# A fused kernel's first block reordered: adaLN columns summed by rows, the S5 branch moved beside the RWKV chain

## The chip, the cores and the metric

One Trainium2 chip, one core. The metric is the device time of one execution, in microseconds (us). The kernel before took 1775.86 us, the median of three runs (1773.12 to 1776.78).

## The reference

The program computes a first block (adaptive norm, input projection, an RWKV-7 time mix beside an S5 state-space mix, output projection, feed-forward) and two further layers of another kind, all in float32 on 512 tokens of width 1024. The change touches the first block only.

```python
ada = silu(c) @ w_ada + b_ada                       # 1024 x 6144
sh_m, sc_m, g_m, sh_f, sc_f, g_f = jnp.split(ada, 6, axis=-1)
h = modulate(rms_norm(x), sh_m, sc_m)               # h * (1 + sc) + sh
proj = h @ w_in                                     # 1792 columns z, 512 columns u
z = z + mu_shift * (z_prev - z)
y_rwkv = rwkv7_time_mix(z, ...)
y_s5 = s5_mix(u, ...)
x = x + g_m * (concatenate([y_rwkv, y_s5]) @ w_out)
h = modulate(rms_norm(x), sh_f, sc_f)
ffn = (silu(h @ w_gate) * (h @ w_up)) @ w_down
x = x + g_f * ffn

# s5_mix: complex powers of abar, then states, then the output
bbar_re = coef_re[..., None] * b_re - coef_im[..., None] * b_im
bbar_im = coef_re[..., None] * b_im + coef_im[..., None] * b_re
_, _, s_re, s_im = lax.associative_scan(_ssm_combine, (a_seq_re, a_seq_im, bu_re, bu_im), axis=0)
y = einsum(c_re, s_re) - einsum(c_im, s_im) + d_skip * ug
zz = gelu(y);  out = zz * sigmoid(zz @ w_glu + b_glu);  out = rms_norm(out) * gain

# rwkv7_time_mix, per token and head
sa = einsum(S, a_t);  S = S * w_t + sa * b_t + v_t * k_t;  y = einsum(S, r_t)
```

## The kernel before, in words

The program is written by hand for each engine. Classes Tensor, Vector, Scalar, Pool and Sync each emit one engine's instructions in their own order (PE, DVE, ACT, POOL and the queue that issues DMAs). They meet on semaphores only, so an instruction that waits holds all that is written behind it on its engine.

**Weights.** All dense weights stream as 234 units of 512 KB, each eight blocks of 128x128, through a ring of four buffers: `Sync.load` (L2794) may fetch unit u+4 when unit u has been eaten. A unit of a dense product is split into a high part (ACT, `unit`, L2035) and a low part (DVE, a subtraction on L1168), and a block is then three matmuls (`mms`, L355). Units in `WHOLE`, those of `w_ada`, are not split.

**First block.** `Tensor.ada_tiles` (L451) makes shift and scale (sh_m, sc_m) from 16 units, each block a matmul with one column; a float32 matmul shows as two instructions in the trace. DVE builds the S5 tables meanwhile (`s5_tables`). Then come the norm h1, the four u tiles of the input projection by rows, the S5 matrices (`s5_matrices`, L514), and a hand-written string ORDER that sets 14 z tiles (`in_proj`, L537) beside the S5 branch (`s5_apply`, L545: the states as a scan on DVE, the outputs yg on PE, a gated unit with dense tiles, a norm). After it `rwkv` (L595) runs: the preparation in two halves, grams (L643), the inverse of unit lower-triangular matrices in five levels (L710), steps (L742) and a scan over eight chunks (L773). The other 32 `w_ada` units are row-summed on DVE beside it (`Vector.ada_columns`, L1333: a scalar times a 128x1024 row added to a sum, L1176), and PE turns each sum into eight columns. Then group norm (L839), output projection (L866), norm h2 and the feed-forward (L879) of 22 tiles.

Helpers record many operations under one line: L350 is every matmul, L353 a transpose, L1168 every tensor-tensor operation of DVE, L1176 its scalar-tensor-tensor, L2592 POOL's tensor-tensor, L2035 ACT's copy, L2032 its other functions. An "arena" is SBUF memory addressed by hand, "b" a PSUM bank, "ring" the raw weights and ring2/ring_55 their low parts, X the residual, H/HR the normed input, cst and par constants, nst the norm's small values.

## Time and profile before

| | |
|---|---|
| median of three runs | 1775.86 us |
| the profiled execution's own time | 1779.91 us |
| its span | 1778.1 us |
| mean granted TensorE clock | 0.928 of full |
| PE busy | 1574.7 us (89%) in 10056 instructions |
| DVE busy | 866.0 us (49%) in 1390 |
| ACT busy | 566.6 us (32%) in 976 |
| POOL busy | 311.4 us (18%) in 245 |
| first matmul of the feed-forward | 574.3 us after the span's start |

Busy is the time in which an engine executed. The profiled execution is 4.05 us above the median, and its own time is 1.8 us over its span. Share of busy time is an average over the whole program, so it says little about the first block, which is the third of the span that is changed.

### The profile page before, as it was taken

What the parts mean: (1) busy time and instruction counts of PE and PEld (TensorE: products, weight loads), DVE (VectorE), ACT (ScalarE), POOL (GpSimd) and SP (SyncE); (2) the same over time, 40 slices, a digit from 0 to 9 for tenths busy, and PEclk for the clock granted to TensorE, in tenths of its full rate; (3) what the DMA queues carried; (4) which work ended last, traced back from release to release, by engine and by line L of the source; (5) the groups of instructions that cost most, each with busy time, mean ns of one, the idle gap of its engine ahead of it and who ended that gap; (6) DMA issues with size and microseconds to landing.
All of it is one profiled execution on the core that took longest, in us unless ns stands there. A gap on an engine that the chain in (4) does not pass through costs nothing.

```text
span 1778.1 us, 23936 instructions
## 1 busy us (share of the span) xinstructions
PE 1574.7 (89%) x10056; PEld 1245.4 (70%) x10056; DVE 866.0 (49%) x1390; ACT 566.6 (32%) x976; POOL 311.4 (18%) x245
## 2 busy tenths in 40 slices
PE   8987697376888999999998999997898989998889
PEld 8875585166866888888886677765676668775767
DVE  7726602876644433332335455445644455444652
ACT  2222114521142322222222443323442443322351
POOL 0000000654110011110001233223210223322110
PEclk9998768689898999999998999999898999999999
DMA  6356103123402222223222111120123112220121
GB/s 248 119 106 84 48 24 95 53 76 127 143 27 81 83 95 95 95 95 124 95 95 83 37 59 60 60 71 25 60 71 113 48 36 75 69 69 26 60 72 70
DMA packets 50362, 141.03 MB, mean 79 GB/s; under 512 B 12624, under 2 KB 17360, under 8 KB 49744
## 3 DMA queue, kind: packets, MB, share of 16 engines
q1 hardware_dynamic: 50256, 139.50, 25.0%
q8 instruction: 80, 1.31, 0.3%
q14 instruction: 26, 0.21, 0.0%
HBM read 134.80 MB, written 4.69 MB: 78 GB/s over the span
## 4 chain that ended last, share of the span: by engine, by line
PE 65%; DVE 10%; ACT 7%; issue 4%; POOL 2%; DMA 1%; SPq 0%; DVEq 0%; ACTq 0%; POOLq 0%
PE b L350 63%; ACT arena L2032 4%; DVE arena L1176 2%; DVE arena L1168 2%; DVE ring L1168 2%; PE b L353 1%; POOL arena L2592 1%; ACT ring L2035 1%; DVE arena L1862 1%; POOL arena L2595 1%; ACT arena L2035 1%; DVE arena L1995 1%; ACT L2032 1%; DVE arena L1820 1%; ACT tile L2035 0%
## 5 line engine op out<-in xcount | busy, mean ns | idle before, releaser
L350 PE MATMUL b<-tile,ring 128*128 128x512 f32 x2288 | 709.2, 405 | 19.8 <-DVE tile L1168 13.3
L350 PE MATMUL b<-HR,ring 128*128 128x512 f32 (+1 forms) x1888 | 631.0, 411 | 69.8 <-DVE ring L1168 41.7
L350 PEld LDWEIGHTS b<-tile,ring 128*128 128x128 f32 x2288 | 442.0, 193 | 128.4 <-issue 10.1
L350 PEld LDWEIGHTS b<-HR,ring 128*128 128x128 f32 (+1 forms) x1888 | 368.6, 195 | 170.1 <-issue 60.3
L1168 DVE TENSOR_TENSOR ring<-ring,ring 128x1024 fp32r<-128x1024 f32 x186 | 255.1, 1372 | 319.8 <-ACT ring L2035 303.6
L350 PE MATMUL b<-arena 64*64 64x64 f32 (+10 forms) x4032 | 306.6, 279 | 44.4 <-issue 29.2
L350 PEld LDWEIGHTS b<-arena 64*64 64x64 f32 (+4 forms) x4032 | 215.6, 153 | 124.7 <-issue 92.2
L2035 ACT ACTIVATE ring<-ring 128x1024 fp32r<-128x1024 f32 x186 | 195.8, 1054 | 219.5 <-PE b L350 205.7
L1168 DVE TENSOR_TENSOR arena<-arena 128x16 f32<-128x16 f32 (+8 forms) x357 | 145.8, 453 | 85.4 <-ACT arena L2032 50.2
L2035 ACT ACTIVATE arena<-b 128x512 f32<-128x512 f32 (+3 forms) x144 | 79.4, 570 | 308.7 <-PE b L350 258.5
L2592 POOL TENSOR_TENSOR arena<-arena 128x256 f32<-128x256 f32 (+4 forms) x76 | 90.8, 1215 | 383.7 <-DVE arena L1168 192.4
L2595 POOL TENSOR_SCALAR arena<-arena 128x128 f32<-128x128 f32 (+1 forms) x64 | 86.9, 1375 | 210.2 <-DVE arena L1867 210.2
L2592 POOL TENSOR_TENSOR tile<-arena,tile 128x512 fp32r<-128x512 f32 x38 | 50.0, 1322 | 396.9 <-ACT tile L2035 396.9
L1168 DVE TENSOR_TENSOR arena<-b,arena 128x512 f32<-128x512 f32 (+3 forms) x78 | 47.8, 630 | 111.3 <-PE b L350 110.0
L2032 ACT ACTIVATE arena<-arena 128x512 f32<-128x512 f32 (+6 forms) x150 | 71.6, 499 | 82.4 <-DVE arena L1172 46.0
L2032 ACT ACTIVATE arena<-b,arena 128x512 f32<-128x512 f32 (+1 forms) x80 | 43.9, 559 | 113.0 <-DVE arena L1172 108.4
L353 PE MATMUL b<-cst,arena 128*128 128x128 f32 (+1 forms) x520 | 66.0, 279 | 13.4 <-POOL arena L2592 12.6
L2035 ACT ACTIVATE tile<-arena 128x512 fp32r<-128x512 f32 x58 | 35.1, 627 | 132.9 <-DVE arena L1168 116.2
L353 PEld LDWEIGHTS b<-cst,arena 128*128 128x128 f32 (+1 forms) x520 | 60.0, 141 | 24.5 <-issue 21.2
L2032 ACT ACTIVATE arena<-b,par 128x512 f32<-128x512 f32 (+1 forms) x50 | 32.8, 686 | 114.2 <-PE b L350 92.2
L350 PE MATMUL b<-ring,HR 128*128 128x512 f32 (+1 forms) x256 | 64.5, 344 | 1.7 <-DVE arena L1179 1.2
L350 PE MATMUL b<-nst,ring 128*128 128x1 f32 x256 | 54.7, 352 | 7.4 <-DMA ring<-in_ws 7.4
(100 smaller groups left out, 981.8 us busy)
## 6 DMA issues: line engine op xcount, KB each, us to landing
ring<-in_ws SPq DMA_DIRECT2D x234, 512.0 KB, 3.5
arena<-in_lw SPq DMA_DIRECT2D x2, 1280.0 KB, 5.5
X<-in_xT SPq DMA_DIRECT2D x1, 2048.0 KB, 12.3
arena<-scr_kpad SPq DMA_DIRECT2D x8, 256.0 KB, 10.5
outT<-X SPq DMA_DIRECT2D x8, 256.0 KB, 2.0
arena<-in_cst SPq DMA_DIRECT2D x1, 1088.0 KB, 4.9
scr_ud<-arena SPq DMA_DIRECT2D x1, 1024.0 KB, 9.1
arena<-scr_ud SPq DMA_DIRECT2D x8, 128.0 KB, 6.1
```

What stands on the lines that cost most here:

```text
L350: return self.e.matmul(out, lhsT, rhs, start=start, stop=stop, skip_group_check=True)
L353: return self.e.transpose(out, in_, self.k.C("ident"))
L1168: return self.e.tensor_tensor(out=out, in0=a, in1=b, op=op)
L1176: return self.e.scalar_tensor_tensor(out=out, in0=a, scalar=s, in1=b, op0=op0, op1=op1)
L1820: self.e.tensor_reduce(out=s_, in_=sq, op=ALU.add, axis=AX.X).then_inc(*dve.inc((l, "sums", q)))
L1862: self.e.tensor_reduce(out=mx[:, q:q + 1], in_=ps[:, o:o + n], op=ALU.max, axis=AX.X).then_inc(*dve.inc((l, "max", h, q)))
L1995: self.e.tensor_reduce(out=mx, in_=Z[:, :, lo:256], op=ALU.max, axis=AX.X).then_inc(*dve.inc((l, "wmax", n)))
L2032: return self.e.activation(out, a, f, scale=scale, **kw)
L2035: return self.e.activation(out, a, ACT.Copy)
L2592: return self.e.tensor_tensor(out=out, in0=a, in1=b, op=op)
L2595: return self.e.tensor_scalar(out=out, in0=a, scalar1=s1, scalar2=None, op0=op0)
```

## The change

Five parts, all ahead of the feed-forward except the end of (3).

1. Six z tiles (`FIRST`) are made by rows in two halves, input rows 0 to 3, then 4 to 7. `w_ada` is reordered to give shift and scale of those halves: group 0 (8 units) is row-summed by DVE (`ada_rows`) before the first half and group 1 between the halves, each turned into eight columns by PE (`ada_sum`) and read by `shift_scale`. The one-column matmuls of `ada_tiles` are gone.
2. The large S5 tables (6 operations of 128x256, 6 of 128x2048, 6 of 128x2304) go from DVE to POOL (`Pool.s5_tables`), whole instead of in quarters. Behind them on POOL come the two small memsets (`z_pad`) that every shifted z tile waits for.
3. Groups 2 to 4 of `w_ada` (24 units) are scaled in place by ACT (`ada_unit`) and added by POOL (128x1024), spread over the RWKV part; group 5 does the same at feed-forward tiles 4 to 11.
4. The string PREP sets the other 12 tiles of the projection (8 z, the four u tiles last) beside `prep`, the RWKV preparation, and the S5 matrices; the string MIX sets grams, inverse, steps and scan (69 steps, "r") beside the S5 branch (33 steps, "s") and the 24 `w_ada` units ("a").
5. The S5 states and inputs live in X's space; x is read from HBM again (`x_again`, 2 MB), and u once more (U2, 1 MB). DVE is started by `par` alone, not `cst`; ACT copies the S5 matrices and u alone.

The order's tables and `Plan`:

```diff
-ORDER = "si" * 3 + "s" * 4 + "ssi" * 8 + "ss" + "i" + "ss" + "i" * 2
-
-WHOLE = set(range(16)) | set(range(36, 68))
-
-Z_ORDER = [12, 13, 4, 5, 6, 7, 0, 1, 2, 3, 8, 9, 10, 11]
+FIRST = [12, 13, 4, 5, 0, 8]
+Z_ORDER = FIRST + [1, 9, 6, 7, 2, 3, 10, 11]
+ADA = [(0, 1, 2, 3, 8, 9, 10, 11), (4, 5, 6, 7, 12, 13, 14, 15), *(tuple(range(n, n + 8)) for n in (16, 24, 32, 40))]
+PREP = "zpzpzpzpzp" + "zmzmpzmpzmpzpzpz"
+MIX = ("s" + "rrr" + "s" + "rrrr" + "srsrsr" + "s" + "rrr" + "rrrs" * 13 + "rs" + "sr" + "rs" * 4 + "r" + "s" + "rrrr" + "s"
...
+def _spread(order, n, last):
+    out, done, r = "", 0, 0
+    for c in order:
+        out += c
+        r += c == "r"
+        while done < n and done * last < n * min(r, last):
+            out, done = out + "a", done + 1
+    return out
+MIX = _spread(MIX, 24, 56)
...
+        self.ZB, self.TMP = R(0, 14, 512), R(84, 2, 516)
+        self.w2, self.g2 = R(88.125, 512), R(24, 512)
+        self.YS, self.Z, self.U2 = R(92, 4, 512), R(100, 4, 512), R(116, 4, 8, 64)
```

`Tensor`:

```diff
     def program(self):
         k = self.k
-        u = k.s("u")
-        for _ in self.ada_tiles():
-            pass
-        self.norm("h1")
-        self.dense_rows([("in", 14 + n) for n in range(4)], self.split_h("h1", True))
-        for n in range(4):
-            self.give(("in", 14 + n), (u, n))
-        self.s5_matrices()
-        parts = {"i": self.in_proj(), "s": self.s5_apply()}
-        for c in ORDER:
-            next(parts[c], None)
-        self.weave((parts["i"], 1), (parts["s"], 1))
-        self.weave((self.rwkv(), 2), (self.ada_columns(), 1))
+        tiles = [("in", n) for n in FIRST]
+        ready = self.split_h("h1", True)
+        self.ada_units(0, range(8))
+        self.token_sums("h1")
+        self.give(("h1", "sums"), (k.s("norm_dve"), ("h1", "mean")))
+        self.spread("h1")
+        self.ada_sum(0)
+        self.dense_rows(tiles, ready, rows=range(4))
+        self.ada_units(1, range(8))
+        self.ada_sum(1)
+        self.give(("h1", "spread"), (k.s("norm_dve"), ("h1", "x", 7)))
+        self.dense_rows(tiles, ready, rows=range(4, 8))
+        for n in FIRST:
+            self.give(("in", n), (k.s("z"), n))
+        self.play(PREP, z=self.in_proj(), p=self.prep(), m=self.s5_matrices())
+        self.play(MIX, r=self.rwkv(), s=self.s5_apply(), a=self.ada_columns())
+        self.ada_sum(4)
         self.group_norm()
         self.out_one()
         self.norm("h2")
...
+    def ada_units(self, g, rows):
+        for r in rows:
+            self.k.order += [("ada", n, r) for n in ADA[g]]
+    def ada_sum(self, g):
+        k = self.k
+        ps = self.take(("ada", g))
+        self.wait_ge(k.s("ada_dve" if g < 2 else "ada_pool"), ("sum", g))
+        for j in range(8):
+            ins = self.mm(ps[:, j:j + 1], k.cols[g][:, j * 128:j * 128 + 128], k.C("ones")[:, 0:1], j == 0, True)
+        ins.then_inc(*k.s("cols_pe").inc(g))
+        self.give(("ada", g), (k.s("ada"), g))
...
-            yield
-        self.give("ada1", (k.s("ada"), 1))
+                self.ada_units(g, [r])
+                if g > 2 and r == 2:
+                    self.ada_sum(g - 1)
...
+            if 4 <= n < 12:
+                self.ada_units(5, [n - 4])
+            if n == 13:
+                self.ada_sum(5)
```

`Vector`:

```diff
-        self.wait_ge(k.s("in0", 16), "cst")
-        self.weave((self.ada_tiles(), 1), (self.s5_tables(), 3), (self.first_squares(), 1))
-        self.ts(k.one_sc, k.ada[:, 8:16], 1.0, ALU.add).then_inc(*k.s("norm_sc").inc(0))
-        self.dense_tiles(4, self.norm_apply("h1", [k.one_sc[:, r:r + 1] for r in range(8)],
-                                            [k.ada[:, r:r + 1] for r in range(8)]))
...
-            self.cp(k.U[:, n, :, :], k.bank["in", 14 + n][:, :].rearrange("p (j t) -> p t j", t=8)).then_inc(*k.s("u").inc(n))
...
-            next(parts[c], None)
-        self.weave((parts["i"], 1), (parts["s"], 1))
-        self.weave((self.rwkv(), 2), (self.ada_columns(), 1))
+        self.wait_ge(k.s("in0", 16), "par")
+        self.weave((self.s5_tables(), 3), (self.ada_rows(0), 1), (self.first_squares(), 1))
+        parts = self.norm_apply("h1", [k.one_sc[:, r:r + 1] for r in range(8)], [k.ada[:, r:r + 1] for r in range(8)])
+        self.dense_tiles(6, parts, 4)
+        for _ in self.ada_rows(1):
+            pass
+        self.shift_scale(1)
+        self.dense_tiles(6, parts, 4)
+        self.ts(k.omm, k.pc("mu", 0, 14), -1.0, ALU.mult, 1.0, ALU.add).then_inc(*k.s("z_omm").inc(0))
+        self.ts(k.omk, k.pc("k_a", 0, 4), -1.0, ALU.mult, 1.0, ALU.add).then_inc(*k.s("prep_dve").inc("omk"))
+        for n in FIRST:
+            self.shifted(n)
+        self.play(PREP, z=self.in_proj(), p=self.prep())
...
+    def ada_rows(self, g):
...
             self.blocks(8)
             yield
...
+    def shift_scale(self, g):
...
+        self.wait_ge(k.s("cols_pe"), g)
+        self.tt(k.ada[:, o:o + 4], ps[:, 0:4], k.pc("b_ada", o, 4), ALU.add).then_inc(*a.inc(("shift", g)))
+        self.stt(k.one_sc[:, o:o + 4], ps[:, 4:8], 1.0, k.pc("b_ada", 8 + o, 4), ALU.add, ALU.add).then_inc(*a.inc(g))
...
-        for ri in range(2):
-            (pa, ca), (pb_, cb) = (((PR, cre), (PI, cim)) if ri == 0 else ((PI, cre), (PR, cim)))
-            for g in range(0, 16, 4):
...
-                self.wait_ge(tab, SOFAR)
-                V(wt[:, 0, gs], powers(pa), weights(ca), ALU.mult)
-                V(wt[:, 1, gs], powers(pb_), weights(cb), ALU.mult)
-                self.wait_ge(tab, SOFAR)
-                if ri == 0:
-                    V(W[:, 0, gs], wt[:, 0, gs], wt[:, 1, gs], ALU.subtract)
-                else:
-                    F(flat(W[:, 1, gs]), flat(wt[:, 0, gs]), -1.0, flat(wt[:, 1, gs]), ALU.mult, ALU.subtract)
-                yield
```

`Scalar`:

```diff
+    def ada_unit(self, g, r):
...
+        self.wait_ge(k.s(f"w{u % RING}", 16), u)
+        if r == 0 and g == 4:
+            self.wait_ge(k.s("cols_pe"), 2)
+        self.af(k.wraw(u) if r else k.cols[g], k.wraw(u), ACT.Copy,
+                scale=k.cact[:, r:r + 1]).then_inc(*k.s("ada_act").inc(("unit", u)))
```

`Pool`:

```diff
-        self.wait_ge(k.s("tab"), "end")
-        self.e.memset(k.KS[0:16, :, 0:112], 0.0).then_inc(*k.s("mat_pool").inc("pad"))
-        self.wait_ge(k.s("u"), 3)
-        self.wait_ge(k.s("mat_act"), ("vm", 14))
-        self.wait_ge(k.s("mat_dve"), ("vm", 12))
+        self.e.memset(k.zero, 0.0).then_inc(*k.s("mat_pool").inc("zero"))
+        self.s5_tables()
         for j in range(2):
             self.e.memset(k.TMP[:, j, 0:1], 0.0).then_inc(*k.s("z_pad").inc(j))
-        for n in range(4):
+        self.blocks(128 + 48)
+        self.play(PREP, p=self.prep())
+        self.blocks(12 * 8)
+        self.play(MIX, r=self.rwkv(), s=self.s5_apply(), a=self.ada_columns())
...
+            V(BB[:, ri], bc(cr, 16), x, ALU.mult)
+            V(t, bc(ci, 16), y, ALU.mult)
...
+        for dst, n, p0, p1, a, b, op in (
+                (VT[:, :, 0], 8, PR, PI, BB[:, 0], BB[:, 1], ALU.subtract),
+                (VT[:, :, 1], 8, PR, PI, BB[:, 1], BB[:, 0], ALU.add),
...
+                (W[:, 1], 9, NPI, PR, cre, cim, ALU.subtract)):
...
+            weights = lambda ap: ap.unsqueeze(2).broadcast_to((128, 16, n, 16))
+            self.wait_ge(tab, SOFAR)
+            V(dst, powers(p0), weights(a), ALU.mult)
+            V(t, powers(p1), weights(b), ALU.mult)
+            self.wait_ge(tab, SOFAR)
+            V(dst, dst, t, op, *(["end"] if p0 is NPI else []))
...
+    def ada_unit(self, g, r):
...
+        u = self.block // 8
+        if r:
+            self.wait_ge(k.s("ada_act"), ("unit", u))
+            self.wait_ge(k.s("ada_pool"), SOFAR)
+            x = k.cols[g]
+            self.tt(x, x, k.wraw(u), ALU.add).then_inc(*k.s("ada_pool").inc(("unit", u), *([("sum", g)] if r == 7 else [])))
...
-                self.tt(h8(k.LL[:, p, :]), h8(k.LT[:, p, :]), level, ALU.mult).then_inc(*inv.inc(("l", l, p)))
...
+                    self.tt(h8(k.LL[:, p, :]), h8(k.LT[:, p, :]), level(l + 1), ALU.mult).then_inc(*inv.inc(("l", l + 1, p)))
+                yield
```

`Sync`:

```diff
         in0 = k.s("in0", 16)
         self.e.dma_start(k.par[:, :], d["par"]).then_inc(*in0.inc("par"))
-        self.e.dma_start(k.cst[:, :], d["cst"]).then_inc(*in0.inc("cst"))
-        for u in range(RING):
-            self.load(u)
-        self.e.dma_start(k.X[:, :, :], d["xT"]).then_inc(*k.s("in1", 16).inc("x"))
+        self.load(0)
+        self.load(1)
+        for i in range(2):
+            self.e.dma_start(k.X[:, 4 * i:4 * i + 4, :], d["xT"][:, 4 * i:4 * i + 4, :]).then_inc(*k.s(f"x_{i}", 16).inc(0))
+        self.load(2)
+        self.load(3)
+        self.e.dma_start(k.cst[:, :], d["cst"]).then_inc(*k.s("cst", 16).inc(0))
...
         self.e.dma_start(k.YS, d["yd"].rearrange("(gt g) c t j -> (g c) gt (t j)", gt=4)).then_inc(*k.s("ys", 16).inc(0))
-        yield
```

**Order, place 1: POOL's first work.** Before, POOL has a memset of 16 partitions and the two z_pad memsets ahead of the preparation of RWKV (ISA sets up the engine; the rows of H are its products):

```order
L2603 MEMSET arena 16x32x112
L2608 MEMSET arena 128x1 x2
L2592 ISA
L2592 TENSOR_TENSOR arena<-arena 128x512 x6
L2592 TENSOR_TENSOR arena<-arena,H 128x512 x2
L2592 TENSOR_TENSOR arena<-arena 128x512 x2
L2592 TENSOR_TENSOR arena<-arena,H 128x512 x2
```

Now:

```order
L2658 ISA
L2658 TENSOR_TENSOR arena<-arena 128x256 x6
L2658 TENSOR_TENSOR arena<-arena 128x16x128
L2658 TENSOR_TENSOR arena<-arena 128x2048
L2658 TENSOR_TENSOR arena<-arena 128x16x128 x2
L2658 TENSOR_TENSOR arena<-arena 128x2048
L2658 TENSOR_TENSOR arena<-arena 128x16x128
L2658 TENSOR_TENSOR arena<-arena 128x2304 x6
L2671 MEMSET arena 128x1 x2
L2658 TENSOR_TENSOR arena<-arena 128x512 x20
L2658 TENSOR_TENSOR arena<-arena,cst 128x512 x8
L2658 TENSOR_TENSOR H<-H,ring 128x1024
```

What moved: 18 table operations stand first on POOL, ahead of the z_pad memsets (128x1 x2) and of the preparation, and the first w_ada add (H<-H,ring) stands behind the grams.

**Order, place 2: DVE before the first norm.** Before, the tables (arena<-arena 128x576 and 128x512) fill DVE up to the first lows of the ring (ring_55<-ring,ring_55), the shift and scale (ada<-b,par) behind them:

```order
L1168 TENSOR_TENSOR arena<-arena 128x512
L1168 TENSOR_TENSOR arena<-arena 128x576 x8
L1176 SCALAR_TENSOR_TENSOR arena<-arena 128x576
L1168 TENSOR_TENSOR arena<-arena 128x512
L1168 TENSOR_TENSOR arena<-arena 128x576 x2
L1176 SCALAR_TENSOR_TENSOR arena<-arena 128x576
L1168 TENSOR_TENSOR arena<-arena 128x576 x2
L1176 SCALAR_TENSOR_TENSOR arena<-arena 128x576
L1168 TENSOR_TENSOR arena<-arena 128x576 x2
L1176 SCALAR_TENSOR_TENSOR arena<-arena 128x576
L1168 TENSOR_TENSOR arena<-arena 128x512 x27
L1168 TENSOR_TENSOR ring_55<-ring,ring_55 128x1024
```

Now:

```order
L1215 TENSOR_TENSOR arena<-arena 128x512
L1219 TENSOR_SCALAR arena<-arena 128x144
L1223 SCALAR_TENSOR_TENSOR arena<-ring,nst,arena 128x1024
L1215 TENSOR_TENSOR arena<-arena 128x512
L1223 SCALAR_TENSOR_TENSOR arena<-ring,nst,arena 128x1024
L1215 TENSOR_TENSOR arena<-arena 128x512
L1223 SCALAR_TENSOR_TENSOR arena<-ring,nst,arena 128x1024
L1215 TENSOR_TENSOR arena<-arena 128x512
L1223 SCALAR_TENSOR_TENSOR arena<-ring,nst,arena 128x1024
L1215 TENSOR_TENSOR arena<-arena 128x512
L1223 SCALAR_TENSOR_TENSOR arena<-ring,nst,arena 128x1024
L1215 TENSOR_TENSOR ring_55<-ring,ring_55 128x1024
```

What moved: the big table operations have left DVE, and rows of w_ada (arena<-ring,nst,arena 128x1024) alternate with 128x512 adds of the first norm's squares.

**Order, place 3: the inverse, levels 0 and on.** Before, DVE alternates there the inverse's adds of a PSUM bank (arena<-arena,b) with rows of w_ada (arena<-ring,nst,arena):

```order
L1176 SCALAR_TENSOR_TENSOR arena<-ring,nst,arena 128x1024 x4
L1168 TENSOR_TENSOR arena<-arena,b 128x512 x4
L1176 SCALAR_TENSOR_TENSOR arena<-ring,nst,arena 128x1024
L1168 TENSOR_TENSOR arena<-arena,b 128x512 x4
L1176 SCALAR_TENSOR_TENSOR arena<-ring,nst,arena 128x1024 x2
L1168 TENSOR_TENSOR arena<-arena,b 128x512 x4
L1172 TENSOR_SCALAR arena<-ring,nst 128x1024
L1168 TENSOR_TENSOR arena<-arena,b 128x512 x4
L1176 SCALAR_TENSOR_TENSOR arena<-ring,nst,arena 128x1024 x3
L1168 TENSOR_TENSOR arena<-arena,b 128x512 x4
```

DVE now (X is where the S5 states live; one step of the S5 scan is four plus four operations):

```order
L1215 TENSOR_TENSOR arena<-X,arena 128x128 x4
L1215 TENSOR_TENSOR X<-X,arena 128x128 x4
L1215 TENSOR_TENSOR arena<-arena,b 128x512 x4
L1215 TENSOR_TENSOR arena<-X,arena 128x128 x4
L1215 TENSOR_TENSOR X<-X,arena 128x128 x4
L1215 TENSOR_TENSOR arena<-arena,b 128x512 x4
L1215 TENSOR_TENSOR arena<-X,arena 128x128 x4
L1215 TENSOR_TENSOR X<-X,arena 128x128 x4
L1215 TENSOR_TENSOR arena<-X,arena 128x128 x4
L1215 TENSOR_TENSOR X<-X,arena 128x128 x4
L1215 TENSOR_TENSOR arena<-arena,b 128x512 x2
L1215 TENSOR_TENSOR ada<-b,par 128x8
```

POOL now:

```order
L2658 TENSOR_TENSOR H<-H,ring 128x1024 x2
L2658 TENSOR_TENSOR ring2f<-arena,cst 128x512 x2
L2658 TENSOR_TENSOR H<-H,ring 128x1024
L2658 TENSOR_TENSOR ring2f<-arena,cst 128x512 x2
L2658 TENSOR_TENSOR H<-H,ring 128x1024
L2658 TENSOR_TENSOR ring2f<-arena,cst 128x512
L2658 TENSOR_TENSOR H<-H,ring 128x1024
L2658 TENSOR_TENSOR ring2f<-arena,cst 128x512 x2
L2658 TENSOR_TENSOR H<-H,ring 128x1024
L2658 TENSOR_TENSOR ring2f<-arena,cst 128x512
```

What moved: the S5 scan's steps (arena<-X,arena and X<-X,arena) stand between DVE's adds of the inverse in place of rows of w_ada, and on POOL each product of a level (ring2f<-arena,cst) has w_ada adds around it.

## Rows read from the trace of the kernel before

**Rows 1.** The page, granted TensorE clock in 40 slices of the span, in tenths.

```profile
PEclk9998768689898999999998999999898999999999
```

**Rows 2.** Windows: start:end length, busy us (count) of PE PEld DVE ACT POOL, clock, DMA share, GB/s.

```profile
0.00:574.30 574.30, 451.75 (x5088) 376.01 (x5089) 323.73 (x607) 158.89 (x232) 87.91 (x63) 0.85 0.34 95
113.40:365.60 252.20, 180.65 (x744) 133.93 (x744) 129.11 (x268) 69.39 (x94) 38.31 (x26) 0.74 0.32 67
365.60:399.00 33.40, 30.96 (x807) 28.15 (x808) 25.21 (x48) 11.52 (x20) 16.90 (x12) 0.93 0.26 84
399.00:463.60 64.60, 47.49 (x1814) 45.54 (x1812) 44.80 (x52) 11.97 (x21) 24.42 (x16) 0.95 0.42 141
463.60:500.70 37.10, 33.92 (x976) 33.03 (x972) 16.69 (x32) 6.47 (x13) 0.00 (x0) 0.86 0.27 88
500.70:574.30 73.60, 61.45 (x232) 45.03 (x233) 37.27 (x51) 30.66 (x44) 5.02 (x4) 0.91 0.20 65
600.00:620.00 20.00, 20.00 (x88) 16.21 (x87) 6.10 (x5) 6.17 (x8) 2.60 (x2) 1.00 0.27 90
211.00:224.00 13.00, 13.00 (x48) 11.14 (x48) 0.00 (x0) 0.00 (x0) 0.00 (x0) 0.50 0.00 0
```

**Rows 3.** Timeline, the start, PE and then DVE: start, us, engine, line, operation.

```profile
7.37 54.75 PE L350 MATMUL b<-nst,ring 128*128 128x1 f32 x256 [7.37 <-DMA ring<-in_ws]
61.98 1.84 PE L350 MATMUL b<-cst,arena 128*128 128x1 f32 x8
...
9.30 0.26 DVE L1168 TENSOR_TENSOR arena<-arena,par 128x16 f32<-128x16 f32 x2 [9.30 <-ACT arena L2032]
...
42.62 17.95 DVE L1168 TENSOR_TENSOR arena<-arena 128x512 f32<-128x512 f32 x27
```

**Rows 4.** Timeline, a later layer, POOL and then DVE.

```profile
1229.02 1.89 POOL L2592 TENSOR_TENSOR arena<-arena 128x1024 f32<-128x1024 f32 x1 [5.80 <-DVE arena L2004]
1242.41 3.60 POOL L2592 TENSOR_TENSOR arena<-arena 128x2048 f32<-128x2048 f32 x1 [11.50 <-DVE arena L2004]
...
1229.49 2.51 DVE L1168 TENSOR_TENSOR ring<-ring,ring 128x1024 fp32r<-128x1024 f32 x1 [0.54 <-ACT ring L2035]
...
1242.88 4.22 DVE L1168 TENSOR_TENSOR ring<-ring,ring 128x1024 fp32r<-128x1024 f32 x1 [0.54 <-ACT ring L2035]
```

**Rows 5.** DVE's line 1168: count, ns min/median/max, first and last start.

```profile
L1168 DVE TENSOR_TENSOR ring<-ring,ring x186: 1204/1226/4223, 60.5 to 1764.9; 128x1024 fp32r<-128x1024 f32 x186
...
L1168 DVE TENSOR_TENSOR arena<-arena,b x48: 673/681/690, 403.4 to 1684.7; 128x512 f32<-128x512 f32 x48
```

**Rows 6.** POOL's line 2592, the same columns.

```profile
L2592 POOL TENSOR_TENSOR arena<-arena x76: 608/742/3602, 297.8 to 1692.6; 128x256 f32<-128x256 f32 x48, 128x512 f32<-128x512 f32 x16, 128x2048 f32<-128x2048 f32 x6, 128x640 f32<-128x640 f32 x4
...
L2592 POOL TENSOR_TENSOR arena<-arena,cst x28: 1263/1278/2258, 372.2 to 448.5; 128x512 f32<-128x512 f32 x28
```

**Rows 7.** DVE's line 1176, rows of w_ada.

```profile
L1176 DVE SCALAR_TENSOR_TENSOR arena<-ring,nst,arena x28: 1272/1284/2280, 316.6 to 473.9; 128x1024 f32<-128x1024 f32 x28
```

**Rows 8.** Timeline of DVE in the S5 branch.

```profile
163.28 5.47 DVE L1168 TENSOR_TENSOR arena<-arena 128x128 f32<-128x128 f32 x16
...
172.76 10.83 DVE L1168 TENSOR_TENSOR arena<-arena 128x128 f32<-128x128 f32 x64
```

**Rows 9.** Timeline of PE: S5 matrices (two rows), then yg.

```profile
93.70 11.20 PE L350 MATMUL b<-arena 64*16 64x128 f32 x128
104.83 3.71 PE L353 MATMUL b<-cst,arena 128*128 128x128 f32 x32
...
210.76 13.32 PE L350 MATMUL b<-arena 128*128 128x64 f32 x48 [4.31 <-DVE arena L1168]
...
230.91 21.91 PE L350 MATMUL b<-arena 128*128 128x64 f32 x96
```

**Rows 10.** Timeline of PE in the RWKV preparation.

```profile
312.45 5.20 PE L350 MATMUL b<-arena 64*128 64x512 f32 x16 [3.24 <-ACT arena L2032]
...
345.75 3.75 PE L350 MATMUL b<-arena,cst 128*128 128x512 f32 x4 [11.43 <-POOL arena L2592]
```

755 lines of the change are left out of this document (420 added, 335 removed).

## The prediction

> **What bounds the kernel now.** I read the whole as stages of the first block, because the change ends where its first feed-forward matmul starts, at 574.3 us of the span; behind it only eight units of w_ada enter. The windows [rows 2] give for the block PE busy 451.8 of 574.3 us at a granted clock of 0.85, against 20.0 of 20.0 us at 1.00 inside the feed-forward (600 to 620). So there are 122 us in which PE has nothing, and more in which it is slow: the page's clock line [rows 1] has 8, 7, 6, 8, 6, 8 in its fourth to ninth slices (133 to 400 us), the projection with the S5 branch beside it and the RWKV preparation. That is the window 113.40 to 365.60: 252 us long, PE busy 181 at clock 0.74. The shortest piece that shows both is 211 to 224 us [rows 2]: PE full, clock 0.50 (the lower of its two levels, 1.2 GHz), 48 small matmuls [rows 9] of the S5 outputs after a wait of 4.3 us for DVE. The start is bound otherwise: 54.75 us of one-column matmuls on PE [rows 3], with the S5 tables on DVE until 60.6 us beside them. The inverse (399.00 to 463.60) is a chain PE, ACT, DVE, POOL over five levels with 12.9 us a level.
>
> A second thing is seen in a later layer [rows 4]. POOL starts a 128x1024 operation at 1229.02 and ends it at 1230.91; DVE starts a subtraction of two SBUF inputs at 1229.49, which takes 2.51 us. With POOL's 128x2048 (3.60 us) it takes 4.22. Alone it takes 1.23, the median of 186 [rows 5]. Both times DVE ends 1.1 us after POOL (1232.00 against 1230.91, 1247.10 against 1246.01): it did nothing until POOL was through. Where one of DVE's inputs is in PSUM, 48 operations lie between 673 and 690 ns [rows 5], some of them in the inverse with POOL at work: those never wait. POOL waits as well: its 128x512 product takes 1278 ns in the median and up to 2258 [rows 6], and rows of w_ada on DVE 1284 and up to 2280 [rows 7]. I read this as exclusion: a POOL operation and a DVE operation with two SBUF inputs run one after the other. This change gives POOL 18 + 24 large operations and leaves two-input operations on DVE beside them, so the two engines' times add where the plan draws them in parallel.
>
> The Trainium skill, "SBUF — State Buffer", section "Who interferes with whom", speaks against this change by the same rule (an exclusive port pair, held for the whole instruction, for a DVE operation with two SBUF inputs beside a GpSimd one that reads SBUF). By it the sum below stands; without it the first rival's time would come out.
>
> **The sum, stage by stage.** Against the span before, from its start to the first feed-forward matmul.
>
> Start, up to the end of the six first tiles. The small S5 tables stay on DVE. Before, DVE starts at 9.30 behind `cst` and goes through the big ones until 60.6 [rows 3]; now `par` alone lets it start about 4 us earlier, and three rows of w_ada (1.28 each [rows 7]) stand between, so I take the tables' end at 21. From there POOL has 18 operations: six of 128x256 at the minimum of 0.61 [rows 6]; eight products with a broadcast input, four of 2048 elements at 3.60 [rows 4] and four of 2304 at 3.60 x 9/8 = 4.05; four sums of two full inputs. For these no row stands: 3.60 is the lower bound, four of the 512-element products, 4 x 1.28 = 5.1 [rows 6], the upper (each with its own start-up), and I take 4.6, and 5.2 for 2304. Together 3.7 + 14.4 + 16.2 + 9.2 + 10.4 = 53.9. Against it stand DVE's two-input operations up to the last row of w_ada: 12 rows at 1.28 = 15.4, one start row 0.75, five adds of 0.67 (17.95 / 27 [rows 3]) = 3.3, three low parts at 1.2 [rows 5] = 3.6, the diagonal 0.7, four low parts of the norm at 0.75 = 3.0: 26.8. Run one after the other: 80.7, to 101.7. In the middle PE does rows 0 to 3 (24 blocks) and then has nothing for about 40 us. Then the column sums (1.84 warm [rows 3], 3.7 at half clock), shift and scale and the norm of row 4, an estimate of 2.8 from three DVE operations near 0.7 and ACT's between: 108.2. Then 24 blocks, three matmuls each at 20.0 / 88 = 0.227 us [rows 2], 0.69 a block: 16.6, with 2 cold: 126.8.
>
> The bounds of this stage: were POOL and DVE independent, the second half would wait for the w_ada rows alone and end near 94.5. With every sum at its upper price it ends 2 us later than I say.
>
> The Trainium skill, "GPSIMD Engine Reference", section "3. Performance versus the Vector engine", gives 4497 ns for an addition of 2048 float32 on GpSimd where the row has 3602 for one with a broadcast input; by the page's figure the twelve large operations would come to 57.3 in place of 50.2 and the whole sum 7 us higher, an estimate.
>
> Projection and preparation. 12 tiles of eight blocks: 12 x 8 x 0.69 = 66.6. The S5 matrices 11.2 + 3.7 [rows 9] = 14.9. The preparation is 32 instructions: 16 in 5.20, 16 between 5.20 / 16 = 0.33 and 3.75 / 4 = 0.94 each [rows 10]; I take 0.56, nearer the lower because dense tiles between them keep PE busy: 14.1. Before, PE waited for it on the other engines again and again (11.43 us for POOL once [rows 10]); dense tiles hide that now, except where the first part waits for tile 13 and the tanh, and the last for the fourth head group: 12 us in all. 66.6 + 14.9 + 14.1 + 12 = 107.6, to 234.4. Bounds: no wait, 222; half of the 71.5 us for which PE was idle in that window before [rows 2] in place of 12, 258. The large gain of the change is here: before, this point was at 365.6.
>
> Grams. Before 33.4 [rows 2]. The four groups of "a" move out (64 small instructions at 0.03, -2.0), the products into the S5 states come in (128 at 0.034, between the 0.026 and 0.038 of the inverse's and the grams' windows, +4.3) and POOL's first three w_ada adds hold DVE's (+2): 37.8, to 272.2.
>
> Inverse. Before 64.6 [rows 2], with 12 DVE rows of w_ada in DVE's idle time. Now for the four levels that have a next one: POOL 16 products at 1.28 [rows 6] = 20.5 and 12 w_ada adds between 1.89 [rows 4] and 2 x 1.28 = 2.56, taken at 2.5, = 30.0. DVE's S5 steps: one is 8 operations, 5.47 / 2 = 2.74 [rows 8], nine of these and the 8.1 of the small ones (10.83 - 2.74, x56 of 64 [rows 8]): 32.8. All of these exclude each other: 83.3. DVE's adds read PSUM and are free of it. Further 14 for the last level, which has no products, and 7 in which the one waits for the other's data: 104.3. Bounds: 64.6, were it all hidden; 20.5 + 30.7 + 32.8 and five levels' chain of half the old length each behind them, about 130. I take the middle because the port would be the busiest thing of the stage by far. To 376.5.
>
> Steps and scan. 37.1 before [rows 2], 3 less without the w_ada column sums; yg comes in here: 144 instructions took 13.32 + 21.91 us [rows 9], so 192 take 47.0; the gated unit's 16 blocks, 11; and 5 of new waits (DVE's last S5 steps and ACT's gelu). 97.1, to 473.6.
>
> Tail: group norm, output projection, norm h2: 73.6 before [rows 2]; the S5 norm's end and the low parts are no longer done ahead, and `ada_sum(4)` waits for POOL's last six adds: +10, bounds 0 and 20. To 557.2, which is 17.1 earlier than 574.3.
>
> Feed-forward: eight w_ada units take ring slots and ACT and POOL time where PE is the bound; the column sum, 1.84, and a unit late once: +3, bounds 2 and 8. The reload of x (2 MB) and U2 run on a DMA share of 0.2 to 0.42 [rows 2] and are costed at nothing: the cover is the scan and the gated unit's tiles; were it gone, the output projection's first result would wait for x. On SP they stand behind the write-back of the outputs, which SP waited for before too, and ahead of the gated unit's loads. The zero fill of kpad waits on SP for POOL's first memset, with the later ring loads behind it; POOL has nothing ahead of that, so nothing is late. The memsets for z_pad are costed at nothing as well, since POOL's tables (to 101.7) end before the first shifted tile.
>
> Sum: -17.1 + 3 = -14.1. The profiled execution took 1779.91, so 1765.8; it was 4.05 above the median of the runs shown, so **1762**.
>
> **The rivals.** *Exclusion costs little* (POOL's and DVE's two-input operations overlap mostly): for it, POOL's w_ada adds and tables could fall in DVE's waits for ACT and PE. Against it, [rows 4]. The start then ends at 94.5 (-32), the inverse at about 69 in place of 104 (-35): with -14 that is -81, 1695. *The inverse becomes the bound and the block slower than before*: in a level, 16/4 products, 3 adds and two S5 steps hold one another, while the chain PE, ACT, POOL waits behind each in turn. A level of 27 us in place of 12.9 makes 135 (+31), by POOL's adds at 2.56, each S5 step split by a POOL operation, and PE's clock falling to its lower level, where the S5 outputs' matmuls took 13.32 / 48 = 0.278 against 0.228 later [rows 9]: 1762 + 31 = 1793. It decides from a level of (104.3 + 14) / 5 = 23.7 us; my own sum has 20.9. For it: PE in the inverse has 47.5 us of work [rows 2], so in 135 us it would be busy a third and the clock line shows what came of that in the preparation. Against it: PE's own work is small there. *In between*, the exclusion half of what I take: 1730, inside my range.
>
> **How the numbers follow.** The sum as above, 0.50, its own range 1740 to 1782 from the bounds (start +2 and -15, preparation -12 and +24, tail +-10, taken as independent). The first rival 0.20, the second 0.30. The range reaches to both: 1700 to 1800. A measurement of this kernel can tell 0.2%, 3.5 us. Within it lie about 0.08, mostly the upper end of the sum; faster: 0.20 of the first rival and 0.40 of the sum, 0.60; slower: the second rival and the rest of the sum, 0.32.
>
> **What would show it.** The windows of the changed kernel: first feed-forward matmul near 557; end of POOL's tables near 90 to 102 and a gap on PE of about 40 us between rows 0 to 3 and 4 to 7; DVE's w_ada rows there with a mean far over 1.28 and POOL's largest operations over 5; the projection and the preparation done near 234, at a clock over 0.9; the inverse over 100 us long with DVE's small operations stretched next to POOL's 128x1024 adds. Wrong would be: DVE rows at 1.28 beside POOL's tables; the inverse at 65 to 75; a wait on x in the output projection or of PE on a ring slot in the feed-forward.

## The result, and the profile after

| | us |
|---|---|
| before, median of four runs (one more than above) | 1775.12 (1773.12 to 1776.78) |
| after, median of four runs | 1855.12 (1852.69 to 1860.64) |
| ratio, 95% interval | 1.0456 (1.0429 to 1.0482) |
| profiled execution of the changed kernel, its span | 1855.85, 1853.9 |
| mean granted TensorE clock | 0.909, before 0.928 |

The change costs 80 us. The forecast was 1762 in a range of 1700 to 1800: outside, and on the other side. The page of the changed kernel (PE's busy tenths, then the granted clock, which answers to [rows 1]):

```profile
PE   0579956579788867799999899998889889998889
...
PEclk9979977766888977899999899999999899999999
```

A slice is 46.3 us here. The clock is better than before in the fourth to sixth slices (139 to 278 us: 9, 9, 7 against 8, 7, 6). It is worse in three of the four behind them (seventh to tenth, 278 to 463 us: 7, 7, 6, 6 against 8, 6, 8, 9). And it has 7, 7, 8 in the 15th to 17th (649 to 788 us), with PE's busy share at 6, 7, 7 tenths: that is the feed-forward, which ran undisturbed before. The windows (columns as in [rows 2]), first the stages up to the first feed-forward matmul at 582.34, then all behind it, then a piece of the feed-forward:

```profile
121.00:226.70 105.70, 97.75 (x490) 73.35 (x489) 58.44 (x69) 58.01 (x82) 32.04 (x20) 0.98 0.19 65
226.00:272.00 46.00, 26.11 (x685) 23.54 (x683) 15.21 (x38) 12.75 (x19) 21.24 (x15) 0.78 0.59 93
272.00:381.40 109.40, 64.26 (x2030) 61.99 (x2026) 94.81 (x183) 36.27 (x49) 61.85 (x34) 0.75 0.50 113
392.00:454.00 62.00, 61.72 (x384) 54.06 (x388) 7.26 (x16) 3.58 (x6) 0.00 (x0) 0.56 0.09 23
454.00:500.00 46.00, 34.53 (x784) 28.80 (x774) 14.58 (x26) 15.97 (x25) 3.83 (x4) 0.89 0.41 131
500.00:582.34 82.34, 66.41 (x253) 48.24 (x251) 41.23 (x56) 32.90 (x46) 5.29 (x5) 0.90 0.17 58
582.34:1853.90 1271.56, 1144.53 (x4984) 883.54 (x4984) 550.36 (x785) 415.90 (x752) 239.33 (x189) 0.94 0.21 71
620.00:840.00 220.00, 171.31 (x659) 135.91 (x658) 53.36 (x41) 49.79 (x63) 33.35 (x21) 0.84 0.24 84
```

The same two last stretches of the kernel before:

```profile
574.30:1778.10 1203.80, 1122.93 (x4968) 869.34 (x4968) 542.28 (x784) 407.74 (x744) 223.46 (x182) 0.96 0.21 72
620.00:840.00 220.00, 220.00 (x953) 178.40 (x952) 67.48 (x60) 62.63 (x80) 24.72 (x19) 1.00 0.30 101
```

Two readings. The first block ends 8 us later than before (582.3 against 574.3), not 17 earlier. And everything behind its end, for which I had +3, takes 67.8 us longer (1271.6 - 1203.8): PE is idle 127.0 in place of 80.9 us and busy 21.6 us more with sixteen matmuls more. In 220 us of feed-forward it gets through 659 matmuls where it did 953.

The timeline there, PE, ACT, DVE and POOL of the changed kernel, from one tile to the next:

```profile
633.69 0.77 PE L395 MATMUL b<-HR,ring 128*128 128x512 f32 x1 [4.78 <-DVE ring L1215]
...
646.51 0.40 PE L395 MATMUL b<-HR,ring 128*128 128x512 f32 x1
653.18 0.77 PE L395 MATMUL b<-HR,ring 128*128 128x512 f32 x1 [6.27 <-DVE ring L1215]
...
673.12 0.76 PE L395 MATMUL b<-HR,ring 128*128 128x512 f32 x1 [6.27 <-DVE ring L1215]
...
647.67 0.63 ACT L2058 ACTIVATE tile<-arena 128x512 fp32r<-128x512 f32 x1 [5.68 <-DVE arena L1215]
648.21 1.13 ACT L2055 ACTIVATE ring<-ring,nst 128x1024 f32<-128x1024 f32 x1
649.25 1.99 ACT L2058 ACTIVATE ring<-ring 128x1024 fp32r<-128x1024 f32 x2
...
646.95 0.69 DVE L1215 TENSOR_TENSOR arena<-b,arena 128x512 f32<-128x512 f32 x1 [12.27 <-PE b L395]
650.32 3.85 DVE L1215 TENSOR_TENSOR ring<-ring,ring 128x1024 fp32r<-128x1024 f32 x2 [2.68 <-ACT ring L2058]
...
649.60 2.35 POOL L2658 TENSOR_TENSOR arena<-arena,ring 128x1024 f32<-128x1024 f32 x1
```

PE ends a tile at 646.9. DVE's product of that tile (646.95) and ACT's copy (647.67) come next, then ACT scales the w_ada unit (648.21), and only then (649.25) does it make the high part of the weights that PE wants; DVE's low part (650.32) follows. PE has waited 6.27 us. POOL has a part in it: its add of the unit just scaled (649.60 to 651.95) stands beside DVE's low part, which takes 2.71 us where it takes 1.23 alone. The first of the eight units has no add, DVE's low parts there take 1.2 each, and PE waits 4.78 (633.69). So about 1.5 us of each of the other seven waits is POOL's and DVE's exclusion, and the rest is the late begin. The code says why it is late: ACT and DVE begin a split ahead of time through `ahead`, which looks at the current unit and the next:

```python
for x in (u, u + 1):
    if x not in self.begun and x not in self.k.whole and x < UNITS:
```

At a tile boundary with a w_ada unit in it, u + 1 is that unit, which is never split. So the next gate unit isn't begun until the products of the tile before are done. It happens at each of tiles 4 to 11: one wait of 4.78 us and seven of 6.27 or 6.28. The page's group of these matmuls, after and then before, has the sum: 45.4 us more of waiting for DVE's low parts.

```profile
L395 PE MATMUL b<-HR,ring 128*128 128x512 f32 (+1 forms) x1888 | 643.6, 417 | 115.7 <-DVE ring L1215 87.1
```

```profile
L350 PE MATMUL b<-HR,ring 128*128 128x512 f32 (+1 forms) x1888 | 631.0, 411 | 69.8 <-DVE ring L1168 41.7
```

This is also what the bubble does to the clock, in two windows of one tile:

```profile
653.18:658.18 5.00, 5.00 (x12) 3.94 (x13) 0.98 (x1) 0.00 (x0) 0.00 (x0) 0.50 0.76 265
658.18:666.86 8.68, 8.67 (x38) 6.71 (x36) 0.00 (x0) 0.60 (x1) 0.00 (x0) 1.00 0.07 28
```

After 6.27 us of nothing PE works 5 us at the lower level, 1.2 GHz (clock 0.50), then at 2.4. The 48 matmuls take 13.7 us in place of 10.9 (48 x 0.227). Eight times 2.8 would be 22, a little too much, since behind the first and the last of the eight the clock of the first 5 us is 0.59 and 0.72. The windows have it directly: 21.6 us more of PE's busy time, and with the 45.4 of waiting that is 67, the whole of the loss.

The start, POOL and three stretches of DVE, answers to [rows 3, 4]:

```profile
19.56 66.25 POOL L2658 TENSOR_TENSOR arena<-arena 128x256 f32<-128x256 f32 x18 [15.77 <-DVE arena L1219]
...
29.17 4.69 DVE L1223 SCALAR_TENSOR_TENSOR arena<-ring,nst,arena 128x1024 f32<-128x1024 f32 x1
33.79 4.68 DVE L1215 TENSOR_TENSOR ring<-ring,ring 128x1024 fp32r<-128x1024 f32 x1
38.40 4.98 DVE L1215 TENSOR_TENSOR arena<-arena 128x512 f32<-128x512 f32 x1
...
80.78 5.66 DVE L1219 TENSOR_SCALAR arena<-ring,nst 128x1024 f32<-128x1024 f32 x1
```

The exclusion is as large as I drew it: a w_ada row of 1.28 takes 4.69, a low part of 1.23 takes 4.68, an addition of 0.67 takes 4.98.

### The profile page after: what moved, and what is told of

It is laid out like the page before. It is cut to its first block, busy times and chain, and to the rows that moved or that the text cites. A ratio compares the mean times of both kernels' runs of the same rounds, so it can differ in the third digit from the quotient of the medians.

```text
span 1853.9 us, 23535 instructions
## 1 busy us (share of the span) xinstructions
PE 1548.3 (84%) x9832; PEld 1218.1 (66%) x9832; DVE 883.9 (48%) x1318; ACT 604.1 (33%) x1017; POOL 434.6 (23%) x291
## 3 DMA queue, kind: packets, MB, share of 16 engines
q8 instruction: 78, 1.28, 0.3%
HBM read 137.95 MB, written 4.69 MB: 77 GB/s over the span
## 4 chain that ended last, share of the span: by engine, by line
PE 64%; DVE 18%; ACT 9%; issue 5%; POOL 2%; DMA 2%; SPq 1%; DVEq 0%; ACTq 0%; POOLq 0%
PE b L395 63%; DVE arena L1215 5%; ACT arena L2055 4%; DVE ring L1215 4%; DVE arena L1223 2%; DVE X L1215 2%; ACT ring L2058 1%; PE b L398 1%; DVE arena L1885 1%; POOL arena L2661 1%; ACT L2055 1%; DVE arena L1219 1%; POOL arena L2658 1%; ACT arena L2058 1%; DVE arena L2018 1%
## 5 line engine op out<-in xcount | busy, mean ns | idle before, releaser
L1215 DVE TENSOR_TENSOR ring<-ring,ring 128x1024 fp32r<-128x1024 f32 x186 | 277.2, 1495 | 302.1 <-ACT ring L2058 301.5
L395 PE MATMUL b<-arena 64*64 64x64 f32 (+10 forms) x3072 | 248.8, 304 | 53.3 <-DVE arena L1215 28.1
L2658 POOL TENSOR_TENSOR arena<-arena 128x256 f32<-128x256 f32 (+5 forms) x102 | 166.0, 1648 | 406.1 <-DVE arena L1215 126.8
L395 PEld LDWEIGHTS b<-arena 64*64 64x64 f32 (+5 forms) x3072 | 162.5, 160 | 126.0 <-issue 84.6
L2058 ACT ACTIVATE arena<-b 128x512 f32<-128x512 f32 (+2 forms) x132 | 71.7, 568 | 228.5 <-PE b L395 192.0
L1215 DVE TENSOR_TENSOR arena<-arena 128x512 f32<-128x512 f32 (+6 forms) x139 | 74.4, 564 | 74.4 <-ACT arena L2055 54.9
L2055 ACT ACTIVATE arena<-arena 128x512 f32<-128x512 f32 (+7 forms) x150 | 71.5, 500 | 71.9 <-DVE arena L1219 46.0
L395 PE MATMUL b<-cst,arena 128*128 128x1 f32 (+1 forms) x200 | 24.8, 281 | 59.1 <-DVE arena L1215 51.0
L395 PE MATMUL b<-X,arena 64*128 64x63 f32 (+1 forms) x320 | 54.1, 343 | 22.2 <-DMA X<-scr_ud 16.8
L2055 ACT ACTIVATE arena<-b 128x512 f32<-128x512 f32 (+1 forms) x44 | 24.7, 561 | 140.1 <-PE b L395 140.1
```

The costliest lines, as they stand in the source:

```text
L395: return self.e.matmul(out, lhsT, rhs, start=start, stop=stop, skip_group_check=True)
L1215: return self.e.tensor_tensor(out=out, in0=a, in1=b, op=op)
L2055: return self.e.activation(out, a, f, scale=scale, **kw)
L2058: return self.e.activation(out, a, ACT.Copy)
L2658: return self.e.tensor_tensor(out=out, in0=a, in1=b, op=op)
```

## The experiments

Fifteen kernels ran, each beside the kernel before on the same chip. For every one, where its stages lie in the span of its profile (us), the time and the ratio to before. The stages are those of one profiled execution; that of before lies 4.1 us above the median of its runs, that of g1 7.0 and that of h2 3.9, the others that ran more than once within 2.8, so a difference of a few us between two rows is not to be read. "Rows" is the first matmul of the first tiles, "chunks" the first 64x64 matmul behind the preparation, "rest" the span behind the first feed-forward matmul (FFN). p1 is made on the changed kernel, m1 and all below it on f1.

```
            rows   chunks  outputs yg     FFN    rest     time     ratio (95%)
before                                    574.3  1203.8
after       61.3   228.5   392.3-449.5   582.3  1271.6  1855.12  1.0456 (1.0429-1.0482)
f1          65.2   228.3   390.3-447.3   583.0  1210.7  1795.05  1.0123 (1.0075-1.0170)
f2          61.3   229.2   392.8-450.0   586.4  1269.1  1857.45  one run
f3          61.3   228.9   391.4-448.3   582.5  1226.7  1811.13  one run
p1          41.8   229.6   395.6-452.7   588.4  1269.5  1861.06  1.0500 (1.0445-1.0555)
m1          61.3   228.5   360.5-421.1   580.0  1210.8  1794.92  1.0136 (1.0092-1.0180)
i2          61.3   228.8   362.8-421.4   554.5  1206.8  1763.23  one run
i3          61.1   229.6   368.7-425.9   562.4  1209.3  1773.64  one run
t0          47.7   201.0   366.4-423.7   559.2  1209.2  1770.33  one run
g1          78.0   217.9   382.2-444.5   579.4  1212.7  1787.00  1.0074 (1.0048-1.0100)
g2          61.2   229.7   386.0-446.3   581.9  1208.0  1791.72  1.0097 (1.0062-1.0132)
g4          77.6   218.0   370.4-430.7   568.0  1206.7  1779.43  1.0037 (1.0014-1.0060)
j1          61.2   228.3   354.9-420.6   557.2  1209.3  1768.42  one run
h1          70.8   211.2   361.9-425.0   561.3  1207.7  1771.86  1.0004 (0.9982-1.0027)
h2          70.5   215.2   348.3-414.0   548.8  1209.2  1756.02  0.9903 (0.9880-0.9927)
h3          70.3   213.7   348.6-408.8   536.6  1207.3  1745.53  0.9842 (0.9820-0.9864)
```

**The feed-forward: f1, f2, f3.** f3 lets `ahead` look past one w_ada unit; f2 counts the two buffers of split weights by split units alone, since a whole unit between two of them made both ask for the same buffer; f1 does both.

```diff
-        for x in (u, u + 1):
+        for x in (u, u + 1, self.k.skip.get(u, u)):     # skip[u] = u + 2 past a w_ada unit
...
-        b = u % 2
+        b = self.nth.get(u, u) % 2                      # nth: number among the split units
```

> The changed kernel, with the split of the next dense unit begun past a w_ada unit in the feed-forward, and the pair buffers counted by dense units alone. Theory 1 (late split): in each of the eight feed-forward tiles with a w_ada unit, PE stands idle (5 to 6.3 us) because ACT's copy and DVE's low part of the next gate unit are begun only behind the tile's own silu and product; with both edits the bubble and the half-clock restart go, 8 x 8 us: about 1792 us. Rival 2 (POOL's adds hold DVE's low parts, exclusion): adds and units are all still there, so within 5 us of 1855. Rival 3 (the ring has too few slots or the queue is late): same, within 5 us of 1855.

> Only the pair buffers are counted by dense units; the split is begun as in the changed kernel. Theory 1: the look-ahead is what is missing, so 1850 to 1857. If buffers alone were the cause: about 1792.

> Only the look-ahead passes the w_ada unit; the pair buffer of the next gate unit is then that of the last up unit, which PE frees at its last block. Theory 1: ACT's copy waits for that block, then 1.05 and 1.2 us of split, ahead of the silu: the bubble falls from 6.3 to about 2.5 us, 1820 to 1835. If the look-ahead alone were the cause: about 1792.

Measured: 1795.05, 1857.45 and 1811.13. The buffers alone give nothing, the look-ahead alone 44 us, both together 60, all of it behind the first block (rest 1271.6 to 1210.7). f1 and f2 came where a late begin had put them (about 1792; 1850 to 1857), f3 is 9 us faster than its range. Rivals 2 and 3 of f1 asked for less than 5 us and fall: the adds and the units are all still there. The windows of f1, to be set beside those above:

```profile
620.00:840.00 220.00, 214.29 (x929) 172.73 (x928) 73.53 (x58) 68.45 (x85) 41.15 (x26) 1.00 0.34 110
582.98:1793.70 1210.72, 1128.00 (x4984) 872.45 (x4984) 551.18 (x785) 416.81 (x752) 240.30 (x189) 0.96 0.23 75
```

With the look-ahead eight w_ada units cost the rest 6.9 us, the upper half of my bounds of 2 and 8. So the cause is shown: not the units, but what their place does to the splits behind them. What is left is 1.2%: between the two profiled spans 15.6 us, of which 8.7 lie in the first block, where 17 less had been forecast, and 6.9 behind it. In f3 each of the eight bubbles is 2.56 us; behind six of them PE goes on at full clock, behind two the first 5 us have 0.66:

```profile
645.28 0.47 PE L396 MATMUL b<-HR,ring 128*128 128x512 f32 x1 [2.56 <-DVE ring L1216]
```

**The start: p1, t0.** p1 holds POOL's tables until DVE has made the norm of row 7, with the z_pad memsets ahead of them. t0 (on f1) cuts the twelve largest table operations to a sixteenth, so the S5 tables are mostly left out.

```diff
         self.e.memset(k.TMP[:, j, 0:1], 0.0).then_inc(*k.s("z_pad").inc(j))
+        self.wait_ge(k.s("norm_dve"), ("h1", "x", 7))
+        self.s5_tables()
```

> The changed kernel, with POOL's 18 table operations held back until DVE has made the norm of the last row; the two small memsets go ahead of them. Theory 1 (exclusion): DVE's rows of w_ada fall to 1.28 each, the six first tiles end at about 97 in place of 121, and the tables run beside the z tiles where DVE's inputs are mostly in PSUM: 10 to 22 us less, 1833 to 1845. Rival 2 (the tables did not hold DVE, the start is bound by loads or ACT): within 4 us of 1855. Rival 3 (preparation then waits for POOL): slower than 1855.

> The kernel of f1 with POOL's twelve large table operations cut to a sixteenth (the rest of the S5 tables is zero). Theory 1 (exclusion at the start): the first column sum of w_ada comes at about 30 us in place of 43.4, the six first tiles end near 91 in place of 121, and the whole is 25 to 30 us shorter, about 1767. Rival 2 (the start is bound by loads and ACT): under 8 us shorter.

In p1 the six tiles start 20 us and their second half 32 us earlier (71.72 against 104.06), and nothing of it is left at the first chunk, 229.6. PE, and POOL beside it:

```profile
71.72 0.76 PE L395 MATMUL b<-HR,ring 128*128 128x512 f32 x1 [3.87 <-DVE tile L1223]
...
140.15 3.57 PE L395 MATMUL b<-arena,cst 128*128 128x512 f32 x4 [32.35 <-POOL arena L2658]
...
76.72 69.24 POOL L2658 TENSOR_TENSOR arena<-arena 128x256 f32<-128x256 f32 x24 [72.86 <-DVE arena L1223]
```

PE waits 32.35 us for POOL's part of the preparation, which stands behind the tables (the 69.24 us hold both). So the expected 1833 to 1845 was missed; it is the third way of the expectation: the price is moved, not avoided. t0 shows the price: without most of the tables the chunks begin 27 us earlier and the feed-forward 24, and its 1770.33 was expected as about 1767.

**The RWKV chain: i2, i3, m1.** All on f1. i2 leaves out 20 of DVE's 21 scan steps of the S5 states, so their outputs are wrong; i3 leaves out all but 16 columns of POOL's w_ada adds, so g_m, sh_f and sc_f are not the reference's; m1 leaves nothing out and moves the 24 adds behind the inverse.

```diff
-MIX = _spread(MIX, 24, 56)
+MIX = _after(MIX, 53, [2, 2, 2, 2, 2, 2, 2, 2, 2, 2, 2, 2])     # m1: two "a" behind each of r 53 to 64
```

> The kernel of f1 without DVE's scan steps over the S5 states (20 of its 21 steps of 8 operations are left out). Theory 1: stretch from grams to the first step product shorter by the steps' own 42 us (14 x 2.6 and 7 x 1.1) and what they waited for POOL, less what was hidden: 30 to 45. Rival 2 (they are hidden in waits for PE and ACT): under 10.

> The kernel of f1 with POOL's w_ada adds outside the feed-forward cut to 16 columns (the rest of each sum is left out); units, scalings by ACT and waits stay. Theory 1 (exclusion): the stretch from grams to the first step product is 20 to 40 us shorter, as in m1. Rival 2: under 8.

> The kernel of f1 (1795) with its 24 w_ada units moved in the order from grams and inverse to behind step 53 of the RWKV chain, beside the S5 outputs. Theory 1 (exclusion in the inverse): POOL's 21 adds at 2.4 us there no longer hold DVE's S5 steps and POOL's own level products: the stretch from the first grams to the first step product (226 to 381 us) is 20 to 40 us shorter; beside the S5 outputs DVE and POOL are idle, but 24 units need 24 x 2.8 us of DMA = 67, so some 0 to 15 come back: 1765 to 1785. Rival 2 (the inverse's length is its own chain and DVE's S5 steps in line, POOL's adds are hidden): within 5 us of 1795. Rival 3 (the ring then bounds the outputs): over 1800.

Against f1, i2 brings the outputs forward by 28 us and the feed-forward by 28; i3 by 22 and 21. Each alone is worth what f1 is too slow by (20.5 us over the kernel before on its chip). i2 stayed just under its 30 to 45 us, i3 came in at the low end of its 20 to 40. What the two do not tell apart is exclusion and standing in line: the steps stand on DVE ahead of the inverse's adds, POOL's adds ahead of its own level products, and to leave them out shortens both lines as well. The longest wait of PE in the inverse of the changed kernel shows both, PE and then DVE:

```profile
363.27 1.99 PE L395 MATMUL b<-arena 64*64 64x64 f32 x64 [13.28 <-DVE arena L1215]
...
348.37 5.97 DVE L1215 TENSOR_TENSOR X<-X,arena 128x16 f32<-128x16 f32 x4
...
362.44 2.48 DVE L1215 TENSOR_TENSOR arena<-arena,b 128x512 f32<-128x512 f32 x4
```

The four operations at 348.37 stand beside POOL's adds and take 5.97 us; the same four take 0.6 right behind them. But from 354.4 to 362.4, with POOL idle, DVE goes through six more steps at their own speed before it comes to the add for which PE waits: that part is the order.

m1 brings the outputs forward by 30 and the feed-forward by 3: 1794.92, not the expected 1765 to 1785. (No run shows the 2.8 us a unit of that expectation; in the changed kernel some landed 1.3 us apart.) DVE, PE and, last, what SP's queue waited for between 300 and 480 us in m1 (us in all, times, longest):

```profile
463.35 2.74 DVE L1233 SCALAR_TENSOR_TENSOR arena<-arena,par 128x512 f32<-128x512 f32 x4 [25.41 <-DMA arena<-scr_yd]
...
470.19 1.86 PE L405 MATMUL b<-arena 64*64 64x64 f32 x29 [26.40 <-DVE arena L1225]
...
SPq L2959 <- POOL H L2668: 103.4, 18, 22.7
```

POOL's adds free the ring slots late, SP's ring loads wait for that in its queue, and behind them stands the write-back and reload of the S5 outputs (scr_yd). DVE waits for these with the RWKV scan's operation in line behind it, and PE for DVE. The gain is given back there, in waits of 25 and 26 us where f1 has one of 8.22 on PE.

**Repairs of one thing each: g1, g2, g4.** g1 makes shift and scale again by one-column matmuls, in the new order of weights, with rows 0 to 7 in one go; g2 puts six adds in the grams and 18 at steps 53 to 58; g4 is both, with the products into the S5 states three gram steps later.

```diff
+        for n in range(16):
+            for r in range(8):
+                ins = self.mm(ps[:, n:n + 1], w, k.cact[:, r:r + 1], r == 0, r == 7)     # g1
...
+MIX = _after(MIX, {2:2, 3:2, 4:1, 6:1, 53:2, 54:2, 55:4, 56:4, 57:4, 58:2})             # g2
```

> The kernel of f1 (1795) with the start's w_ada part undone: shift and scale come from 128 one-column matmuls on PE as before, the six first tiles run over all eight rows in one go; the tables stay on POOL. Theory 1 (at the start DVE's rows of w_ada and POOL's tables exclude each other, PE waits): PE's columns end near 62 as before, rows start at 70 and the 48 blocks end near 104 where the changed kernel needs 121: 12 to 20 us less, 1775 to 1783. Rival 2 (the tables alone hold the norm, whoever makes the columns): within 6 us of 1795.

> The kernel of f1 with the 24 w_ada units placed by hand: 6 in the grams (where PE waits for the S5 inputs' transfer), none in the inverse, 18 beside the S5 outputs, four to a group of outputs, which is what the ring holds. Theory 1: as in m1 the first step product comes near 344 in place of 379, and now the scan is not held behind the loads, so the gain stays: 1760 to 1772. Rival 2 (the order of the units does not matter, what is won in the inverse is lost behind it in any case, as in m1): within 6 us of 1795.

> All edits: f1, PE's columns at the start, the w_ada units as in g2, and the products into the S5 states three gram steps later, so that PE has grams to do while the S5 inputs arrive (it waits 17 us there). If the gains add: 1795 - 17 - 28 - 8 = 1742, with 10 either way; faster than the kernel before (1775). If the three share a cause: 1755 to 1770.

g1 starts the first tiles 13 us later and ends the preparation 10 us earlier than f1; the ratio falls from 1.0123 to 1.0074, intervals that just overlap. At 1787.00 it misses its 1775 to 1783. g2 (1.0097) can't be told from f1, the second way of its expectation: the inverse ends 13 us earlier, PE then waits 10.86 us for DVE's S5 states in place of 5.11, and the wait of the grams for the S5 inputs is 20.3 us in place of 14.8. Together they give 1.0037, more than either, but 1779.43 lies above both ranges of its expectation (about 1742; 1755 to 1770): the wait for the states stays at 10.68 us, and its third edit did not shorten the wait for the S5 inputs, 15.3 us.

**What bounds the rest: j1, h1, h2, h3.** j1 is g2 with all but one of the S5 scan steps left out. h1 is g4 with the large tables back on DVE, woven into the time in which PE sums w_ada. h2 also makes the u tiles before the last two z tiles and lets SP write and reload the S5 inputs during the preparation (and takes the state products back to their first place). h3 is h2 with DVE's operation on the returned S5 outputs two scan steps later.

```diff
-PREP = "zpzpzpzpzp" + "zmzmpzmpzmpzpzpz"
+PREP = "zpzpzpzmpzmpm" + "zzpzmpzpzpzzp"                     # h2, h3
-        for n in Z_ORDER[6:] + [14, 15, 16, 17]:
+        for n in Z_ORDER[6:12] + [14, 15, 16, 17] + Z_ORDER[12:]:
...
-... "rrrr" + "s" + "rr" + "sr" * 4 + "ss"
+... "rrrrrr" + "sr" * 4 + "sss"                              # h3, the end of MIX
```

> g2 (1791.7) with DVE's scan steps over the S5 states left out but for one. Theory 1 (in g2 DVE's S5 steps are the bound of the stretch up to the outputs, so the adds' gain was hidden behind them): both gains come out together, the outputs start near 340 in place of 386: 1735 to 1750, below i2 (1763.2) by 12 to 25. Rival 2 (the adds were never in the way beside the steps): at i2's 1763 within 6.

> g4 (1779.4) with the large tables back on DVE, in whole pieces, beside PE's one-column matmuls. Theory 1 (POOL's tables hold the norm's DVE operations also there): the first dense block starts near 70 in place of 77.6, the whole is 6 to 10 us shorter: 1769 to 1774. Rival 2 (in place of POOL's, DVE's own 50 us of tables end too late for the norm): 1779 or more.

> h1 with the four u tiles ahead of the last two z tiles and the transfers of the S5 inputs issued right behind them. Theory 1 (PE waits for the transfer, on the path): the wait of 15 us before the products into the states falls to 0 to 5, 8 to 14 us less: 1757 to 1765. Rival 2 (DVE's grams and the inverse behind them set the pace): within 4 us of h1.

> h2 with the step in which DVE waits for the outputs' transfer placed two scan steps later. Theory 1 (the scan's state stands behind that wait on DVE's queue, 8 to 9 us): 3 to 8 us less than h2, about 1755, faster than the kernel before by 1%. Rival 2 (the gated unit behind it is then as much later): within 3 us of h2.

j1's outputs begin 8 us earlier than i2's and its feed-forward 3 us later. It took 1768.42, near its rival's 1763 and far from 1735 to 1750: a single run each, and by them the adds cost as much beside the outputs as they had in the inverse. h1 undoes the move of the tables and takes another 7 us off (568.0 to 561.3), as expected; the ratios, 1.0037 and 1.0004, have intervals that overlap. h2 takes 12.5 off, by the medians 15.8, a little more than its 8 to 14: the wait of the grams for the S5 inputs is gone (none of the three edits was run alone). h3 takes 12.2 more, by the medians 10.5, where 3 to 8 were expected. DVE at the same place, first in h2, behind a wait for the DMA:

```profile
432.42 2.74 DVE L1224 SCALAR_TENSOR_TENSOR arena<-arena,par 128x512 f32<-128x512 f32 x4 [9.29 <-DMA arena<-scr_yd]
```

and in h3, without one:

```profile
429.29 0.42 DVE L1216 TENSOR_TENSOR arena<-b,nst 128x256 f32<-128x256 f32 x1 [6.11 <-PE b L393]
429.63 2.73 DVE L1224 SCALAR_TENSOR_TENSOR arena<-arena,par 128x512 f32<-128x512 f32 x4
```

h3 took 1745.53 us (1741.14 to 1749.86), 0.9842 of before (0.9820 to 0.9864): 1.6% faster than the kernel before, and faster than the changed one. Its windows and its clock line:

```profile
0.00:536.60 536.60, 446.80 (x5073) 379.68 (x5073) 293.16 (x534) 189.12 (x265) 128.96 (x84) 0.87 0.36 100
536.60:1743.90 1207.30, 1120.90 (x4984) 866.83 (x4984) 550.91 (x785) 416.66 (x752) 240.46 (x189) 0.97 0.23 75
...
PEclk9999998656998999999998999998998999999999
```

The block is 38 us shorter than before. What the eighth to tenth slices still show (305 to 436 us, clock 6, 5, 6) is the end of the inverse and then the S5 outputs, behind a wait of 10.65 us for DVE's states; that wait was not attacked.

## Why the prediction was wrong, point by point

**The failed step: the feed-forward, "+3, bounds 2 and 8".** It measured +67.8. I counted the eight w_ada units' ring slots and their ACT and POOL time, and took "a unit late once". I did not ask, at each place where a unit enters, which split is begun ahead there: the diff puts a whole unit on every tile boundary, the one place where ACT and DVE have a chain of their own in front of the next split. With f1 the term is 6.9. The last sentence of my list, a wait of PE in the feed-forward, named the right place and the wrong resource: it waited for the low part, not for a ring slot. Some 1.5 us of each of seven waits was the exclusion itself, which I had drawn for the start and the inverse and not for here. This is 65 of the 93 us by which the forecast missed.

**Second: "Steps and scan, 97.1".** It measured 118.6 (381.4 to 500.0). The outputs took 13.32 + 10.86 + 11.12 + 13.35 = 48.7 for my 47.0. The rest is waits, for which I had 5: 5.35 for DVE's states and 8.04 for the scan, and the stretch's clock of 0.56, at which the RWKV matmuls between the outputs run as well. The two long ones on PE, and DVE's behind the second:

```profile
392.28 13.32 PE L395 MATMUL b<-X,arena 128*128 128x64 f32 x48 [5.35 <-DVE X L1215]
...
473.83 1.86 PE L395 MATMUL b<-arena 64*64 64x64 f32 x29 [8.04 <-DVE arena L1215]
...
466.99 2.74 DVE L1223 SCALAR_TENSOR_TENSOR arena<-arena,par 128x512 f32<-128x512 f32 x4 [7.25 <-DMA arena<-scr_yd]
```

The second is DVE's own wait for scr_yd, passed on. I had placed that round trip through HBM on SP's queue and priced it at nothing, and did not list what stands behind the wait on DVE. h3 shows its price: 12 us in the profiles, 10.5 by the medians.

**Grams, 37.8:** 48.1 (228.5 to 276.6). The wait for the S5 inputs was not in the sum:

```profile
260.32 1.98 PE L395 MATMUL b<-X,arena 128*64 128x64 f32 x32 [16.84 <-DMA X<-scr_ud]
```

The u tiles come last, and their way out to HBM and back is 17 us longer than the work between. The order made that visible; I read past it.

**Right within the bounds of their terms.** The start, in its total: the tiles ended at 121 for 126.8, POOL's tables at 85.8 for 101.7, since fewer of DVE's two-input operations than I summed fell beside them: seven of group 1's rows came after their end. The gap between the halves was 16 us (88.5 to 104.1), not 40, since the exclusion had already held up the first half (column sums at 43.4, a wait of 6.55 inside). Preparation: 107.5 for 107.6, at clock 0.98. Tail: 82.3 for 83.6. The exclusion holds: the rows of the start show it, and t0, which takes POOL's side of it away, gives 24 us; with the inverse at 104.7 and not 69, the first rival (it costs little) falls.

**Right in part by luck: the inverse, 104.7 for 104.3.** The total is met, its parts are not. POOL's adds took 2.40 us for 2.5, but the stage held 16 of them and not 12 (38.3 us for 30.0). DVE did 17 steps there, worth about 40 us at the medians of their operations (0.39, 0.19 and 0.36 us) for my 32.8, and they took about 77 beside POOL. Part of both lay in the last level, which I had priced at 14 us with nothing beside it. Put into the same rule, these would have given about 120 us; it adds all of both engines' work, and part of it lay where the other was idle.

Together the stages make +25.1 over the forecast at the first feed-forward matmul; with the +64.8 behind it that is 89.9 of the 90.05 between 1765.8 and the profiled 1855.85, and the last 3 us are that this execution lay 0.7 over its median where that of before lay 4.05 over.

**The rivals.** The second, slower through the inverse, had the sign and not the mechanism: it asked for a level over 23.7 us, and the inverse took 104.7, 20.9 a level. That f1 lands at its 1793 is chance. No rival was set in the feed-forward.

The Trainium skill, "SBUF — State Buffer", section "Who interferes with whom", had been the rule against this change, and the traces agree with it: 4.69 us beside POOL for a w_ada row of 1.28. The same section says that `tensor_scalar` may enter a mode that takes both port pairs and then contends too, which my list of contenders (two SBUF inputs) left out; the 5.66 us below agree.

## What to carry to other kernels

A look-ahead of fixed depth is part of the schedule: before a new kind of work is put between its items, look at each place for what is then no longer begun ahead, and for buffers numbered by position. Where two engines exclude each other, sum their times; here work moved from one to the other saved nothing (h1), and moving it in time (p1, m1, g2) only moved the wait. For every wait that an order creates, DMA round trips first, write down what stands behind it on its engine and on the queue that issues it: here two of them were worth between 10 and 16 us each (h3, h2).

## What the runs showed of the hardware that was not expected

DVE's one-input operations are held by POOL too. In the changed kernel's line 1219 (count, ns min/median/max, first and last start):

```profile
L1219 DVE TENSOR_SCALAR arena<-ring,nst x2: 747/3202/5658, 9.5 to 80.8; 128x1024 f32<-128x1024 f32 x2
```

The first of the two had POOL idle and took 0.75, the second, beside the tables, 5.66. In p1 two of 128x512 take 8.00 us where they take 0.48 each alone. Operations with an input in PSUM stay at their time in the same stretches (0.73 to 0.75 for `arena<-X,nst,b`).

POOL's own tables: 66.25 us for 18 operations beside DVE's w_ada rows, 57.60 in g4, where DVE has less to do; I had summed 53.9 for them alone. In g4 the sums of two full inputs of 128x2048, for which the prediction had no row and took 4.6, took 4.50 and 4.51, the products 3.67 for 3.60.

The clock after a bubble: behind six of the eight waits of the changed kernel (all of 6.27 or 6.28 us, full clock before) the first 5 us ran at the lower level, behind the other two at 0.59 and 0.72. One such tile lost 2.8 us on top of its 6.27, 1.4 times the wait. Behind f3's waits of 2.56 us six times nothing was lost and twice the first 5 us had 0.66; elsewhere in the same kernels waits of 2.1 to 3.1 us behind full clock were followed now by 1.00, now by 0.66 to 0.72 (the changed kernel at 1599.02: 2.55 us, then 0.66; at 1673.86: 3.05 us, then 1.00). So a short bubble costs at least its length, and the runs here do not tell when it costs more.
